# Latent mixer: rotary query rows as two tiles of halves, a 64-column key projection in full precision, values behind the queries

## What is computed

```python
def apply_rope(t, cos, sin):
    t1, t2 = jnp.split(t.astype(jnp.float32), 2, axis=-1)
    return jnp.concatenate([t1 * cos - t2 * sin, t2 * cos + t1 * sin], axis=-1)

def even_mixer(h, cos, sin, w_in, pool_w, pool_scale, q_norm, w_q_up, kv_norm, w_kv_up, w_out):
    z = h @ w_in                                   # 512 + 256 + 128 + 32 columns
    u, cq, ckv, kr = jnp.split(z, [512, 768, 896], axis=-1)
    y_pool = pool_mixer(u, pool_w, pool_scale)
    q = (rms_norm(cq, q_norm) @ w_q_up).reshape(B, S, 8, 96)       # 64 plain + 32 rotary
    kv = (rms_norm(ckv, kv_norm) @ w_kv_up).reshape(B, S, 8, 128)  # 64 keys + 64 values
    q_rope = apply_rope(q[..., 64:], cos, sin)     # 8 heads, 32 rows each
    k_rope = apply_rope(kr, cos, sin)              # one key of 32 rows for all heads
    y_att = mla_causal_attention(q_nope, q_rope, k_nope, k_rope, v)
    return jnp.concatenate([y_pool, y_att], axis=-1) @ w_out
```

## Time and profile before

| what | value |
|---|---|
| median of 3 runs | 3227.89 us (3225.61 to 3229.62) |
| the profiled execution, its own time | 3221.78 us |
| span of the profiled execution | 3220.5 us |
| PE busy | 3212.8 us, 100% |
| DVE, ACT, POOL busy | 1568.5, 1095.6, 1330.0 us |
| instructions | 36641 |

### The profile page before, as it was taken

How to read it: one execution, slowest core, us unless ns; L and a number is a source line. 1 busy time by engine, 2 the same in 40 slices (tenths; PEclk the granted TensorE clock), 3 DMA queues, 4 the chain that set the end, 5 groups by cost and what they waited for, 6 DMA issues and landing times.

```text
span 3220.5 us, 36641 instructions
## 1 busy us (share of the span) xinstructions
PE 3212.8 (100%) x14930; PEld 2672.1 (83%) x14930; DVE 1568.5 (49%) x1859; ACT 1095.6 (34%) x1473; POOL 1330.0 (41%) x551
## 2 busy tenths in 40 slices
PE   9999999999999999999999999999999999999999
PEld 7888888888888888888888877888888888988888
DVE  6441276554234431576544268545544486454421
ACT  4222333322222223433222355543223475432222
POOL 4444433544454444434444433225444213154443
PEclk9999999999999999999999999999999999999999
DMA  4223322332232322322332322323223223232322
GB/s 153 98 99 103 118 79 73 111 98 98 94 110 98 99 98 98 115 79 87 104 99 95 111 90 75 120 97 103 98 94 101 99 96 134 92 105 98 98 92 85
DMA packets 93239, 321.58 MB, mean 100 GB/s; under 512 B 10512, under 2 KB 14992, under 8 KB 93072
## 3 DMA queue, kind: packets, MB, share of 16 engines
q1 hardware_dynamic: 87680, 312.07, 29.3%
q10 hardware_dynamic: 5392, 7.17, 0.7%
HBM read 316.05 MB, written 2.10 MB: 99 GB/s over the span
## 4 chain that ended last, share of the span: by engine, by line
PE 99%; ACT 0%; DVE 0%; issue 0%; ACTq 0%; DVEq 0%
PE bank L381 20%; PE bank L385 20%; PE bank L382 20%; PE bank L396 9%; PE bank L397 9%; PE bank L403 9%; PE bank L366 1%; PE bank L367 1%; PE bank L370 1%; PE bank L722 0%; PE bank L855 0%; PE bank L849 0%; PE bank L850 0%; PE bank L581 0%; PE bank L573 0%; PE bank L574 0%
## 5 line engine op out<-in xcount | busy, mean ns | idle before, releaser
L2625 POOL TENSOR_TENSOR wlo<-raw,whi 128x1024 fp32r<-128x1024 f32 x535 | 1326.5, 2489 | 1870.0 <-ACT whi L1037 1869.8
L1037 ACT ACTIVATE whi<-raw 128x1024 fp32r<-128x1024 f32 x588 | 612.3, 1052 | 597.5 <-PE bank L403 411.4
L381 PE MATMUL bank<-gxh,whi 128*128 128x512 f32 x1536 | 600.2, 391 | 0.0
L382 PE MATMUL bank<-gxl,whi 128*128 128x512 f32 x1536 | 597.7, 389 | 0.0
L396 PE MATMUL bank<-gxh,whi 128*128 128x512 f32 x1248 | 487.6, 391 | 0.9 <-ACT whi L1037 0.9
L397 PE MATMUL bank<-gxl,whi 128*128 128x512 f32 x1248 | 485.7, 389 | 0.0
L381 PE MATMUL bank<-f_hh,whi 128*128 128x512 f32 x1034 | 402.2, 389 | 0.0
L382 PE MATMUL bank<-f_hl,whi 128*128 128x512 f32 x1034 | 402.2, 389 | 0.0
L385 PE MATMUL bank<-gxh,wlo 128*128 128x512 f32 x1536 | 379.6, 389 | 0.0
L1864 DVE TENSOR_TENSOR f_u<-bank,R 128x512 f32<-128x512 f32 x132 | 91.2, 691 | 583.1 <-PE bank L403 583.1
L381 PEld LDWEIGHTS bank<-gxh,whi 128*128 128x128 f32 x1536 | 288.4, 188 | 61.0 <-issue 0.7
(11 more groups left out here) (431 smaller groups left out, 3675.9 us busy)
## 6 DMA issues: line engine op xcount, KB each, us to landing
raw<-stream SPq DMA_DIRECT2D x588, 512.0 KB, 3.3
xa_mem<-memT ACTq DMA_DIRECT2D x2, 1024.0 KB, 6.2
m_dk<-decay ACTq DMA_DIRECT2D x2, 514.0 KB, 4.7
x<-xT ACTq DMA_DIRECT2D x4, 256.0 KB, 5.2
x<-xT SPq DMA_DIRECT2D x4, 256.0 KB, 6.7
outT<-x SPq DMA_DIRECT2D x2, 512.0 KB, 3.0
m_ct<-cos ACTq DMA_DIRECT2D x2, 256.0 KB, 2.7
m_sn<-sin ACTq DMA_DIRECT2D x2, 256.0 KB, 3.0
```

What stands on the lines that cost most here:

```text
L381: pe.matmul(out, seq(hi, k, P), h, start=first and k == 0, stop=False)
L382: pe.matmul(out, seq(hi, k, P), l, start=False, stop=False)
L1037: act.activation(M.whi[r][:, :], M.raw[r][:, :], ACT.Copy).then_inc(*S.tick("hi", u))
L2625: pool.tensor_tensor(M.wlo[r][:, :], M.raw[r][:, :], M.whi[r][:, :].bitcast(F32), ALU.subtract).then_inc(*S.tick("lo", u))
```

## The change

It does these things:

- The rotary rows of all eight heads' queries are cut in halves of 16. One tile of 128 rows holds one half of each head, a second tile the other (which half is in which tile alternates from head to head). No swapped copies are computed. DVE makes four products and two sums of the two tiles. The results lie in `rot` and `pt1_start`. So the queries take six tiles (two rotary, four plain) where they took eight. The second query unit's last four column groups are zeros and unused.
- The rows of a head lie in two tiles, so they go to `Q` by two DMAs of 16x512 for each head: 16 DMAs where there were eight of 32x512. SP issues them all behind the key's DMA, after a wait for that DMA, and `scores(0)` waits for all of them.
- The key's unit has its 64 columns (32 and the swapped 32) at the front, and is not split in high and low parts. ACT scales eight 128x64 pieces of it by the norm's gain into `K`, and PE multiplies them with `x` in float32, even channel blocks into PSUM rows 0 to 63, odd ones into rows 64 to 127. DVE scales both and adds them with one more instruction. POOL has no work for this unit.
- The value tiles come behind the first four query tiles, on PE and on ACT. Query tiles four and five go to banks 7 and 3.

```diff
+    def turned_keys(key, out):
+        u = U[key]
+        w = M.m2["K"]
+        pe.wait_ge(*S.at("hi", u))
+        for k in range(0, KD, 2):
+            for e in range(2):
+                mm = pe.matmul(out[64 * e:64 * e + 64, :], seq(w, k + e, 64), seq(M.x, k + e),
+                               start=k == 0, stop=k == KD - 2)
+        mm.then_inc(*S.tick("used", u))
...
-        project(("m2", 1), next_bank("rk")[:, :])
+        turned_keys(("m2", 1), next_bank("rk"))
...
+        u = open_unit(("qup", 0))
+        for n in range(4):
+            query_tile(n, u, n)
+        ring[0] += 4
+        token_latents()
+        u = open_unit(("qup", 1))
+        for n in range(4, 6):
+            query_tile(n, u, n - 4)
 
         def scores(h):
-            pe.wait_ge(*S.at("qnope", h // 4, h % 4))
-            pe.wait_ge(*S.at(f"qr{h // 4}", 3))
+            pe.wait_ge(*S.at("qnope", h))
             if h == 0:
+                for half in range(2):
+                    pe.wait_ge(*S.at(f"qr{half}", MLA_HEADS - 1))
                 pe.wait_ge(*S.at("kr2"))
...
+        if u == PLAIN:
+            gain = gain_after(M, M2_STAGE - 1)
+            for k in range(KD):
+                act.activation(seq(M.m2["K"], k, 64), M.raw[r][:, k * P:k * P + 64], ACT.Copy, scale=gain(k)).then_inc(
+                    *S.tick("hi", u))
+            return
...
+        plain_queries(0)
+        plain_queries(1)
+        for n in range(NB):
+            act.wait_ge(*S.at("kv_up", NB + n) if n < NB - 1 else S.at("used", U[("kvup",)]))
+            act.activation(seq(T["V"], n), bank[5 + n % 2][:, :], ACT.Copy).then_inc(*S.tick("V", n))
+        ahead(("qup", 1))
+        plain_queries(2)
+        plain_queries(3)
+        pooled_hi(0)
...
-        dve.tensor_tensor(rk, bank[BANK["rk"]][:, :], Rn[:, :], ALU.mult).then_inc(*S.tick("rk"))
+        dve.tensor_tensor(rk[64:P, :], bank[BANK["rk"]][64:P, :], Rn[64:P, :], ALU.mult).then_inc(*S.tick("rk_odd"))
+        dve.tensor_tensor(tmp[64:P, :], bank[BANK["rk"]][0:64, :], Rn[0:64, :], ALU.mult).then_inc(*S.tick("rk"))
...
         dve.wait_ge(*S.at("rk"))
+        dve.tensor_tensor(rk[64:P, :], rk[64:P, :], tmp[64:P, :], ALU.add).then_inc(*S.tick("rk_sum"))
+        dve.wait_ge(*S.at("rk_sum"))
...
     def turned_queries(half):
         sp.wait_ge(*S.at("rot_q", half))
-        for e in range(4):
-            sp.dma_start(M.m2["Q"][64:96, (half * 4 + e) * SEQ:(half * 4 + e + 1) * SEQ],
-                         M.m2["rot"][32 * e:32 * e + 32, 0:SEQ]).then_inc(*S.tick(f"qr{half}", e, by=16))
+        for h in range(MLA_HEADS):
+            row = 64 + 16 * ((h + half) % 2)
+            sp.dma_start(M.m2["Q"][row:row + 16, h * SEQ:(h + 1) * SEQ],
+                         M.m2["pt1_start" if half else "rot"][16 * h:16 * h + 16, :]).then_inc(
+                *S.tick(f"qr{half}", h, by=16))
...
+            sp.wait_ge(*S.at("kr2"))
             turned_queries(0)
-        if u == U[("poolw",)]:
-            sp.wait_ge(*S.at("kr2"))
             turned_queries(1)
```

More of the change, by code:

```diff
@@ L693, in mixer2, with token_latents @@
                 *S.tick("kv_up", pair))
[L694 to L701, removed]
+        def token_latents():
+            u = U[("kvup",)]
+            for n in range(NB):
+                b = claim(5 + n % 2, "V", n)
+                ts = slice(n * P, (n + 1) * P)
+                wide = slice(4 * P, 8 * P)
+                pe.matmul(b[:, :], T["ch2"][:, ts], M.whi[u % SLOTS][:, wide], start=True, stop=False)
+                pe.matmul(b[:, :], T["ch2"][:, ts], M.wlo[u % SLOTS][:, wide], start=False, stop=False)
+                mm = pe.matmul(b[:, :], T["cl2"][:, ts], M.whi[u % SLOTS][:, wide], start=False, stop=True)
+                mm.then_inc(*S.tick("kv_up", NB + n) if n < NB - 1 else S.tick("used", u))
@@ L702, in mixer2, with query_tile @@
+        def query_tile(n, u, e):
+            emptied = ("rot_a", "rot_b", ("qnope", 1), ("qnope", 3), ("qnope", 5), ("qnope", 7))[n]
+            b = claim(q_bank(n), *(emptied if n > 1 else (emptied,)))
+            for k in range(2):
+                mm = product3(b[:, :], u, slice((2 * e + k) * P, (2 * e + k + 1) * P), T[f"ch{k}"], T[f"cl{k}"], k == 0,
+                              k == 1)
+            mm.then_inc(*S.tick("q_up", n) if n in (0, 1, 2, 4) else S.tick("used", u))
         for j in (0, 1):
@@ L703, in mixer2 @@
             pe.wait_ge(*S.at("latent", j))
-        for half in range(2):
-            u = open_unit(("qup", half))
-            for e in range(4):
[L707 to L711, removed]
+        u = open_unit(("qup", 0))
@@ L1245, in mixer2, with plain_queries @@
             act.wait_ge(*S.at("latent", j))
[L1246 to L1255, removed]
+        def plain_queries(pair):
+            act.wait_ge(*(S.at("used", U[("qup", pair // 2)]) if pair % 2 else S.at("q_up", 2 + pair)))
+            for e in range(2):
+                h = 2 * pair + e
+                act.activation(T["Q"][0:64, h * SEQ:(h + 1) * SEQ], bank[q_bank(2 + pair)][e * 64:e * 64 + 64, :],
+                               ACT.Copy).then_inc(*S.tick("qnope", h))
+        plain_queries(0)
+        plain_queries(1)
+        for n in range(NB):
+            act.wait_ge(*S.at("kv_up", NB + n) if n < NB - 1 else S.at("used", U[("kvup",)]))
[4 more added lines that the diff above has]
+        pooled_hi(0)
         scale = QK ** -0.5
@@ L1633, in bank_plan @@
         out["knope", pair] = ring.next()
-    for half in range(2):
-        for e in range(4):
-            out["q", half, e] = ring.next()
+    for n in range(4):
+        out["q", n] = ring.next()
+    out["q", 4], out["q", 5] = 7, 3
     out["pool", 0], out["pool", 1], out["pool", 2], out["pool", 3] = 3, 7, 3, 3
@@ L1671, in p_bank, with q_bank @@
     return BANK["pool", j]
-def q_bank(half, e):
-    return BANK["q", half, e]
+def q_bank(n):
+    return BANK["q", n]
 def vector_program(dve, S, M):
@@ L2716, in stream @@
     swap = np.concatenate([kr[:, 16:32], kr[:, 0:16]], 1)
[L2717 removed]
+    kr = np.concatenate([kr, swap, np.zeros((D, 64), np.float32)], 1)
     u = m_tiles(u)
```

52 lines of the change are left out of this document (26 added, 26 removed).

## The result

| | before | changed |
|---|---|---|
| median | 3225.62 us (7 runs, 3224.30 to 3229.98) | 3236.77 us (7 runs, six of them 3234.43 to 3239.05) |
| the profiled execution, its own time | 3221.78 us | 3236.82 us |

The ratio of the runs is 1.0031, with a 95% interval of 1.002 to 1.0041, and the medians are 11.15 us apart: the changed kernel is slower. The seventh run of the changed kernel, 8504.02 us at a mean granted clock of 0.529, was disturbed, and nothing is read from it.

A forecast was written before the change was run, and what follows sets the result against it. PE bounds the kernel; its first scores, waiting for sixteen query DMAs on SP, come 6.8 us later, plus 2.5 for a slowed clock: 3227.89 + 9.3 = 3237.2 us, range 3231.5 to 3240.5.

The forecast's parts named there:

- Key's unit, 3.64 us: On PE, four pairs of float32 matmuls at 0.91 us, halves running together, 3.64 us instead of 5.46.
- Rival D: On PE, the key's column halves don't run together, so the key comes 3.3 us later: 3238.6 us, chance 0.06.
- PE's small waits, 1.5 and 0.8: PE waits 1.5 us for bank 0 ahead of the first query tile, about 0.8 for bank 5 in the values.
- The reciprocal, 0.14 later: On DVE, one more instruction ahead of the reciprocal makes it 0.14 us later, bounds 0 and 0.61.
- The key's DMA, 0.86 later: On SP, the key's DMA is issued 0.86 us later, at 1905.33, with 0.72 for DVE's sum of blocks.
- Landing 4.8, issues 0.625, landing 2.0: On SP, key's DMA lands in 4.8 us, sixteen issues take 0.625 each, the last lands 2.0 later; scores 6.8 later.
- Rivals B and C: SP's issues cost by rows, 0.31 us each: 3232.5, chance 0.15; or are nearly free, not slower: 3225.4, chance 0.04.
- The clock, 2.5 us, bounds nothing and 3.5: On PE, scores and projection behind the 9.3 us wait run at a slowed clock, adding 2.5 us, bounds nothing and 3.5.
- Rival A: On PE, the same wait ahead of the first scores but the clock stays, no slow stretch: 3234.7 us, chance 0.15.

The follow-up runs named there:

- e3: Changed kernel with ACT's rounding of unit m2,5 moved behind the value copies: 3236.57 us against 3227.91 before the change, ratio 1.0028.
- e1: Changed kernel with query DMAs issued head by head, each head's scores waiting for its own two: 3229.41 us against 3227.91 before the change, ratio 1.0007.
- e2: Changed kernel with 48 throwaway matmuls on PE ahead of the first scores' wait: 3239.89 us against 3227.91 before the change, ratio 1.004.
- e7: Kernel before with only the key's part of the change; queries, values and DMAs as before: 3226.13 us against 3225.74, ratio 1.0004.
- e10: Changed kernel with the value tiles back ahead of the query tiles on PE and ACT: 3232.83 us against 3222.16 before the change, ratio 1.0031.
- e4: Changed kernel with SP waiting for the key's DMA only before head 7's query DMA, not before the first: 3237.15 us, one execution.
- e8: Changed kernel with the second tile's eight query DMAs issued on ACT's queue instead of SP's: 3232.91 us, one execution.
- e5: Changed kernel with the edits of e1, e3 and e4 together: 3224.21 us against 3225.74 before the change, ratio 0.9993.
- e6: e5 with two value tiles ahead of the query tiles and two behind the first four: 3221.57 us against 3225.74 before the change, ratio 0.9993.
- e9: e6 with pool-branch work behind the first head's maxima on DVE and first exponentials on ACT: 3219.07 us against 3222.16 before the change, ratio 0.9985.

## Why the prediction was right, and where it was off

The time (3237.2 against 3236.77 us) and the sign were right, and the mechanism was the one forecast. Step by step:

- **Key's unit, 3.64 us.** Measured 3.66. Rival D is out.
- **PE's small waits, 1.5 and 0.8.** Measured 1.78 and 0.56. The last block of the queries starts at 1914.57 and has three matmuls of 0.23, so PE was ready for the scores at about 1915.25, 27.4 us behind the norm sum, where 26.8 was forecast (1912.3 - 1885.54).
- **The reciprocal, 0.14 later.** Measured (1896.28 - 1887.81) - (1893.55 - 1885.54) = 0.46. The two scalings are 0.73 us apart, not 0.61.
- **The key's DMA, 0.86 later.** This is the step that failed. It was 3.3 us later (22.2 against 18.9): 0.46 for the reciprocal, 0.72 for the sum, and 2.1 that the step left out, the stretched L2148. The prediction had POOL's work down as "an engine that waits", and never asked when its next subtraction would start once ACT's order was changed. Edit e3 takes it out and gets 2.14 back.
- **Landing 4.8, issues 0.625, landing 2.0.** Measured 4.89 to the next issue, 0.63 and 2.0. Rivals B and C are out: an issue of 16 rows costs what one of 32 does. e1, which keeps the issues and only stops waiting for the last fourteen, gets back 10.6 of the 12.8 us, 9.0 of it at the first scores and 1.6 in the clock.
- **The clock, 2.5 us, bounds nothing and 3.5.** The granted clock was 0.50, and it cost 3.3. Rival A is out here; e2 shows that it would have been right with PE kept busy.

So the local sum was 12.8 us, where 6.8 + 2.5 = 9.3 was forecast: 3.5 too small, 2.1 of it the collision and 0.8 the clock. The time still came out because of the base. The forecast was added to 3227.89, the median of three runs; with seven runs that median is 3225.62, so the base was 2.27 too high. The medians moved by 11.15, which is 1.85 more than the 9.3 forecast. The two errors cancel but for 0.4 us. Nor do the medians show all of the 12.8: what the earlier stage adds differs from run to run, and it added less to the changed kernel's median (2.34 above its lowest run) than to that of before (3.84 above the profiled execution). The lowest run of the changed kernel, 3234.43, is 12.65 above that execution of before, close to the local 12.8. The number was partly luck, the chain was not.

## What to carry to other kernels

Count DMAs that one queue must issue ahead of a wait as time, and let each consumer wait for its own alone: here this was worth 10.6 of 12.8 us. An issue of 32 KB cost as much as one of 64. When work is taken from an engine or moved, look at what the engines behind it do earlier: less PE work turned into waits for ACT (e7), and an earlier rounding on ACT sent POOL into DVE's chain. A wait of PE costs more than its length where the clock falls with it: e7 removed 1.8 us of work, met a wait of 2.16, and its third head came 2.1 us later than before.

## What the runs showed of the hardware

- **Clock.** PE's granted clock fell to 0.50 around waits of 2.1 to 2.2 us in the mixer (e1, e7, e10), where the prediction had thought of one of 9 us only. It cost 1.7 us in e1, and as much by estimate in e7; after this change's long waits it cost more: 2.4 to 3.8 behind 7.7 to 11.1 us (the changed kernel, e3, e4, e8, e10). In the mixer it did not fall around 1.8 and 0.6 (e5), nor around 0.9 and 1.3 (e6). Nor does the length of a wait decide it alone: the changed kernel's wait of 2.20 us at 1435.52 left it at 1.00, and the same place in e5, 2.21 us, took it to 0.56. Of the ten waits of 2.2 us in the earlier stages of all twelve traces, seven took it down to 0.50 to 0.56 and three left it at 1.00.
- **POOL beside DVE.** A DVE instruction of 0.7 us with both inputs in SBUF takes 2.5 to 2.8 us beside one 2.4 us subtraction on POOL that started first. This seems to be behind the 2.27 us of the earlier stage too. There, DVE's two products start at 1417.52 in the changed kernel:

```profile
1417.52 3.78 DVE L2033 SCALAR_TENSOR_TENSOR m_cg<-m_z,lcol,m_cg 128x512 f32<-128x512 f32 x2
```

  In the kernel before they start at 1417.48, and take 2.24 us less:

```profile
1417.48 1.54 DVE L1994 SCALAR_TENSOR_TENSOR m_cg<-m_z,lcol,m_cg 128x512 f32<-128x512 f32 x2
```

  POOL starts a subtraction just as the second of the two is due: the second is recorded at 1418.31 and POOL at 1418.35 with the change, 1418.26 and 1418.31 before. So the records put DVE first by 0.04 and 0.05 us, and yet only the one with the change is stretched, to 2.99 us; what decides is finer than they show. At the same place in e9 DVE keeps its 1.54 us, and POOL's subtraction takes 2.96 us in place of 2.39. The twelve traces fit: the pair takes 3.8 us here, or at the same code some 930 us earlier, ten times, and each time PE has a wait of 2.2 us behind it; where the pair takes 1.54, PE has none. Runs of one and the same kernel also fall into groups: 12 of the 19 runs of before in e9's comparison lie at 3221.72 to 3222.30 us, three at 3225.75 to 3228.08, four at 3229.68 to 3229.78. That these places make the groups fits, but was not tried.
- **Issues.** 0.63 us for each DMA from SBUF to SBUF behind another on the same queue, of 32 or of 64 KB, on SP and on ACT (e8). SP's eight took 5.00 us beside ACT's, and 4.98 alone; one burst of eight took 5.92 (e2), cause open.
